# Splitting h straight from the normalised input, and three pieces of shift and scale added up on VectorE

## The chip, the cores and the metric

One core of one Trainium2 chip runs the whole program. The metric is the device time of one execution in microseconds (us).

## What is computed

One diffusion step of a single trunk layer, for 128 context tokens and 256 latent tokens (T = 384 in all) of 2048 channels. Each of the two token sets has its own conditioning vector, and from it six vectors of 2048 (shift 1, scale 1, gate 1, shift 2, scale 2, gate 2). All numbers are float32. The change is in the first three lines of the layer:

```python
def ada_modulation(cond, w_ada, b_ada):
    m = jax.nn.silu(cond) @ w_ada + b_ada
    return [p[:, None, :] for p in jnp.split(m, N_MOD, axis=-1)]
...
    sh1, sc1, g1, sh2, sc2, g2 = ada_modulation(cond, w_ada, b_ada)
    h = rms_norm(x, g_norm1) * (1 + sc1) + sh1
    proj = h @ w_in
    q, k, v, bg, cg, u = jnp.split(
        proj, [D_ATTN, D_ATTN + D_KV, D_ATTN + 2 * D_KV, D_ATTN + 2 * D_KV + D_CONV,
               D_ATTN + 2 * D_KV + 2 * D_CONV], axis=-1)
```

Behind them come attention and a short convolution, the output projection, a router and sixteen experts, whose weights (some 400 MB) are read once.

## The kernel before

**Matrix products in two parts.** h and the weights of the projections are each split into a high part (rounded to the narrower format fp32r) and a low part (the rest), and TensorE forms three products of the parts. For the weights `hi_part(u)` on ScalarE writes the high part of unit u (`w_part(u, 0)`) and `lo_part(u)` on VectorE subtracts it from the raw unit (`w_part(u, 1)`). Unit u of 1 MB holds two chunks of 128 rows of `w_in` for the queries, so units 0 to 7 serve the chunks k = 0 to 15; units 8 to 11 hold four chunks of keys and values each. For h, `hp[:, 0, k]` is the high part of chunk k and `hp[:, 1, k]` the low part, each 128 x 384.

**Shift 1 and scale 1 first.** They come in three blocks of channels: chunks 0 to 5, 6 to 11, and 12 to 15 (`BLOCKS`). The rows of `w_ada` for a block arrive in pieces (`PIECES`): 16 of 768 KB for each of the first two blocks (pieces 0 to 15, 16 to 31), and 8 of 1 MB, each with two chunks of 128 rows, for the last (pieces 32 to 39). TensorE multiplies a piece by the conditioning (`piece(n)` there) into bank 0 and adds one to `w_used`. Buffers are few: the load of piece n waits until `w_used` has reached `PIECE_FREE[n]`, or until the piece before it in its buffer has been read.

**The order around the change is written out by hand.** SyncE issues the loads in the order of `START_LOADS` (a number is a piece, "u5" is unit 5); each waits in the queue behind the one before. TensorE runs the query products chunk by chunk, each of three token tiles t = 0, 1, 2 with 6 matmuls of 512 columns, and behind (k, t) the pieces of `PIECES_AT`. When a block's pieces are multiplied, VectorE copies the rows out (`start_rows`), TensorE turns them (`turn_start`), and VectorE makes shift and gain of the block's chunks. Block 1 is turned behind (5, 1), block 2 behind (11, 0). Where TensorE would stand still in the first block, `idle_work` issues products that nobody reads: 5 behind each of the pieces 8 to 15 and 12 behind the first turn.

**h_block.** Both ScalarE and VectorE have a function of this name, called for each block. VectorE's `h_even` makes the even chunks of h in place in `xhatT`, ScalarE makes the odd ones in place and then copies both to the high parts; VectorE subtracts to get the low parts (`h_parts_ready`). The two chunks of a pair are made together. In between, behind the first pair, stands one `lo_part` (unit 1 in block 0, unit 4 in block 1) and its `hi_part`. Behind block 2, ScalarE issues seven small loads and then does `hi_part(7)`, for which `lo_part(7)` and the products of k = 14 wait.

## Time and profile before

| what | us |
|---|---|
| median of 3 runs | 1526.53 |
| lowest and highest | 1525.94, 1527.6 |
| the profiled execution, its own time | 1527.68 |
| its span | 1526.0 |
| TensorE busy | 1448.4 |
| VectorE busy | 602.4 |
| ScalarE busy | 255.1 |

All stretches below are in microseconds from the span's start. Queries are computed from 53.6 to 146.1, then come keys, values and the convolution with attention until about 570, the router around 596 to 603, and the experts to the end. A busy time of TensorE counts matmuls that overlap; what tells more is the start of a group of matmuls beside the start of the next.

### The profile page before, as it was taken

Reading aid. Unit: us, or ns where it says so; the run is one execution under the profiler, and the core shown is the slowest. Engines: PE = TensorE matmul, PEld = TensorE weight load, DVE = VectorE, ACT = ScalarE, POOL = GpSimd, SP = SyncE. Lnnn points to the kernel's source line nnn. Section 1 sums busy time; section 2 is a strip of 40 time slices with the busy share of each in tenths; the row PEclk is TensorE's granted clock in tenths of the full one; section 3 lists DMA queues with packets and bytes.
Section 4 is the critical chain, followed back from the end, with each engine's and each line's share of the span. In section 5 each row is a group of like instructions: output and inputs, shape, how many; then the busy total and the mean of one; then the engine's idle time right before and its main releaser. Section 6 shows DMA issues by size and latency. Waiting matters only on the chain.

```text
span 1526.0 us, 18551 instructions
## 1 busy us (share of the span) xinstructions
PE 1448.4 (95%) x7856; PEld 882.8 (58%) x7856; DVE 602.4 (39%) x1019; ACT 255.1 (17%) x358; POOL 26.7 (2%) x58
## 2 busy tenths in 40 slices
PE   6999999999999999999989989889889899999998
PEld 3667788888889997435425335335335335335433
DVE  4433977978768986101301301301301201211313
ACT  4223223333233223000000000000000000000200
POOL 0000000000000000000000000000000000000000
PEclk8999999999999999999999999999999999999999
DMA  9999788777787659999999999999999999999999
GB/s 373 403 392 328 263 325 315 267 258 262 277 293 274 220 192 367 368 434 432 431 431 432 429 433 431 433 431 429 435 429 433 431 433 432 428 433 430 432 421 344
DMA packets 99264, 572.48 MB, mean 375 GB/s; under 512 B 9533, under 2 KB 54533, under 8 KB 76677
## 3 DMA queue, kind: packets, MB, share of 16 engines
q1 hardware_dynamic: 87824, 520.14, 83.4%
q0 software_dynamic: 6912, 50.33, 8.6%
q10 hardware_dynamic: 4468, 1.14, 0.3%
q8 instruction: 45, 0.74, 0.2%
q14 instruction: 15, 0.11, 0.0%
HBM read 565.02 MB, written 6.55 MB: 375 GB/s over the span
## 4 chain that ended last, share of the span: by engine, by line
PE 67%; DMA 23%; DVE 5%; SPq 2%; issue 2%; ACT 1%; ACTq 0%; DVEq 0%
PE psum L638 65%; DMA ring<-in_w_up 19%; SPq L551 2%; DMA res<-in_w_ada 1%; DMA ring<-in_w_ada 1%; DVE res L1615 1%; DVE w_parts L1505 1%; DMA ring<-in_w_down 1%; SPq L441 1%; PE psum L648 0%; PE psum L824 0%; PE psum L1076 0%; DVE stat L1575 0%; DVE hid L1574 0%; PE psum L1046 0%
## 5 line engine op out<-in xcount | busy, mean ns | idle before, releaser
L638 PE MATMUL psum<-ring,hid 128*64 128x512 f32 x3024 | 681.2, 598 | 52.9 <-DMA ring<-in_w_up 39.7
L638 PEld LDWEIGHTS psum<-ring,hid 128*64 128x64 f32 x3024 | 240.8, 138 | 469.8 <-issue 411.7
L1941 DVE TENSOR_TENSOR hid<-psum,hid 128x512 f32<-128x512 f32 x16 | 11.1, 692 | 517.2 <-PE psum L638 517.2
L638 PE MATMUL psum<-h_parts,w_parts 128*128 128x384 f32 x1152 | 207.3, 337 | 1.3 <-DVE mix L1648 1.3
L638 PEld LDWEIGHTS psum<-h_parts,w_parts 128*128 128x128 f32 x1152 | 199.9, 188 | 5.1 <-issue 2.5
L1505 DVE TENSOR_TENSOR w_parts<-ring,w_parts 128x2048 fp32r<-128x2048 f32 x52 | 119.1, 2290 | 76.5 <-ACT w_parts L1205 76.3
L1205 ACT ACTIVATE w_parts<-ring 128x2048 fp32r<-128x2048 f32 x52 | 99.6, 1916 | 208.8 <-PE psum L638 177.9
L638 PE MATMUL psum<-w_parts,h_parts 128*128 128x512 f32 x432 | 103.9, 395 | 2.1 <-DVE h_parts L1549 1.3
L638 PE MATMUL psum<-ring,early 128*32 128x512 f32 (+4 forms) x694 | 96.5, 536 | 7.6 <-DMA ring<-in_w_ada 6.5
L638 PEld LDWEIGHTS psum<-w_parts,h_parts 128*128 128x128 f32 x432 | 79.5, 188 | 27.8 <-issue 10.3
L638 PEld LDWEIGHTS psum<-early,mix 128*128 128x128 f32 x768 | 86.6, 192 | 9.0 <-issue 9.0
L638 PE MATMUL psum<-early,mix 128*128 128x128 f32 x768 | 88.6, 276 | 0.8 <-DVE early L1886 0.8
L1421 ACT ACTIVATE hid<-psum 64x1024 f32<-64x1024 f32 x24 | 24.4, 1018 | 334.9 <-PE psum L638 334.7
L638 PE MATMUL psum<-hid 128*128 128x384 f32 (+1 forms) x248 | 77.7, 465 | 0.0
L1615 DVE SCALAR_TENSOR_TENSOR res<-res,early 128x2048 f32<-128x2048 f32 x30 | 69.2, 2346 | 11.3 <-issue 6.5
L638 PE MATMUL psum<-attn_parts,w_parts 128*128 128x384 f32 x384 | 68.3, 335 | 0.0
L638 PE MATMUL psum<-conv_parts,w_parts 128*128 128x384 f32 x384 | 67.9, 335 | 0.0
L638 PEld LDWEIGHTS psum<-attn_parts,w_parts 128*128 128x128 f32 x384 | 66.6, 188 | 1.1 <-issue 0.8
L638 PEld LDWEIGHTS psum<-conv_parts,w_parts 128*128 128x128 f32 x384 | 66.5, 188 | 0.8 <-issue 0.8
L1933 DVE SCALAR_TENSOR_TENSOR res<-psum,mod,res 128x128 f32<-128x128 f32 x192 | 63.0, 409 | 0.8
L638 PEld LDWEIGHTS psum<-hid 128*128 128x128 f32 x248 | 45.7, 190 | 30.4 <-issue 5.7
L1414 ACT ACTIVATE hid<-psum 128x512 f32<-128x512 f32 x16 | 9.6, 597 | 271.7 <-PE psum L1046 158.4
(216 smaller groups left out, 754.0 us busy)
## 6 DMA issues: line engine op xcount, KB each, us to landing
ring<-in_w_up SPq DMA_DIRECT2D x30, 4096.0 KB, 23.2
ring<-in_w_gate SPq DMA_DIRECT2D x28, 4096.0 KB, 29.9
ring<-in_w_down SPq DMA_DIRECT2D x26, 4096.0 KB, 30.0
ring<-in_w_ada POOLq DMA_DIRECT2D x48, 1024.0 KB, 7.5
ring<-in_w_in SPq DMA_DIRECT2D x36, 1024.0 KB, 8.1
ring<-in_w_ada SPq DMA_DIRECT2D x28, 768.0 KB, 15.5
res<-in_w_ada SPq DMA_DIRECT2D x16, 1024.0 KB, 6.2
ring<-in_w_out SPq DMA_DIRECT2D x16, 1024.0 KB, 5.6
```

The lines of the kernel that those rows point to most:

```text
L441: sp.dma_start(piece_buf(n).rearrange("p (m n) -> p m n", m=2), src).then_inc(piece_in[PIECE_SEM[n]], 16)
L551: sp.dma_start(tail_slot(b, e)[:, 2 * half:2 * half + 2, :], down_pairs(e, 1, half)[:, :, col:col + width])\
L638: return nc.tensor.matmul(out, lhsT, rhs, start=start, stop=stop, skip_group_check=True)
L1205: return nc.scalar.activation(out, in_, ACT.Copy)
L1414: nc.scalar.activation(act.rearrange("p (a b) -> p a b", a=4), bank[3 if first and e == 0 else 0][:, :].rearrange("p (b a) -> p a b", a=4) ...
L1421: last = nc.scalar.activation(y_sb[half][row:row + ES, :].rearrange("p (b n) -> p b n", b=2), psum[row:row + ES, 2:4, :], ACT.Copy, scale= ...
L1505: tt(w_part(u, 1), raw_unit(u), w_part(u, 0).bitcast(F32), ALU.subtract).then_inc(lo_ready, 1)
L1615: stt(added_up_3[n], chunk_3, cond[:, k, n:n + 1], added_up_3[n], ALU.mult, ALU.add).then_inc(add_done_3, 1)
L1933: last = stt(xT[:, k, lo:hi], bank[b][:, lo:hi], mod3[:, 5 * KC + k, n:n + 1], xT[:, k, lo:hi], ALU.mult, ALU.add)
L1941: tt(by_row, bank[1][:, :].rearrange("p (b a) -> p a b", a=4), by_row, ALU.mult).then_inc(act_ready, 1)
```

## The change

It has three parts. First, ScalarE no longer makes chunks of h in place: it writes the high part of every chunk straight from `xhatT` (scale, shift and rounding in one operation, one for the 128 context tokens and one for the 256 latent ones), while VectorE makes the same chunk in float32 in one of four places in `tmp` (`h_full`) and subtracts, also in two operations per chunk; TensorE's tile t = 0 waits for the context half alone. Second, pieces 33, 35 and 37 are no longer multiplied on TensorE: VectorE multiplies them by the two conditioning vectors and adds them up in `added_up_1` (`piece_add`), and TensorE sums the result over the partitions behind piece 39 (`piece_sums`). Third, there is less idle work: none behind piece 15, and 6 behind the first turn.

```diff
-    [24, 25, 26, 28] + list(range(33, 37))
-
-START_LOADS = [*range(12), "u0", *range(12, 19), "u1", *range(19, 24), "u2", *range(24, 28), "u3", *range(28, 34), "u4", 34, 35, "u5", 36, 37, "u6", 38, 39, "u7"]
+    [24, 25, 26, 28] + [33, 0, 34, 0]
+ADDS_FREE = {37: 4, 39: 8}
+
+PIECES_ADDED = [33, 35, 37]
+PIECES_USED = len(PIECES) - len(PIECES_ADDED)
...
-             (6, 2): [32, 33], (7, 2): [34], (8, 2): [35, 36], (9, 2): [37], (10, 2): [38, 39]}
+             (6, 2): [32], (7, 2): [34], (8, 2): [36], (10, 2): [38, 39]}
...
-IDLE_FROM, IDLE_PIECE, IDLE_H = 8, 5, 12
+SUMS_AT = (10, 2)
+IDLE_FROM, IDLE_PIECE, IDLE_H = 8, 5, 6
...
+            def piece_sums():
+                pe.wait_ge(ones_set, 3)
+                pe.wait_ge(piece_added, 4 * len(PIECES_ADDED))
+                width = BLOCKS[2][1]
+                for n in range(2):
+                    for j in range(4):
+                        at = j // 2 * width + j % 2 * width // 2
+                        last = mm(bank[0][32 * j:32 * j + 32, 0:width // 2], add_rows_of[:, 1 - n:33 - n], added_up_1[n][:, at:at + width // 2], False, n == 1)
+                last.then_inc(w_used, 1)
...
-                if n >= IDLE_FROM:
+                if IDLE_FROM <= n < PIECE_ENDS[0] - 1:
...
-                pe.wait_ge(h_parts_ready, k + 1)
                 for t in range(NT):
+                    if t < 2:
+                        pe.wait_ge(h_parts_ready, 2 * k + t + 1)
...
-                for k in range(first_k + 1, end_k, 2):
+                for k in range(first_k, end_k):
                     for n, (lo, hi) in enumerate(COLS):
-                        last = nc.scalar.activation(xhatT[:, k, lo:hi], xhatT[:, k, lo:hi], ACT.Identity,
-                                                    scale=gain[:, 0, k, n:n + 1], bias=mod3[:, k, n:n + 1])
-                    last.then_inc(h_act, 1)
-                    a.wait_ge(h_dve, k // 2 + 1)
-                    copy(hp[:, 0, k - 1, :], xhatT[:, k - 1, :]).then_inc(h_hi, 1)
-                    a.wait_ge(h_act, k // 2 + 1)
-                    copy(hp[:, 0, k, :], xhatT[:, k, :]).then_inc(h_hi, 1)
+                        nc.scalar.activation(hp[:, 0, k, lo:hi], xhatT[:, k, lo:hi], ACT.Identity,
+                                             scale=gain[:, 0, k, n:n + 1], bias=mod3[:, k, n:n + 1]).then_inc(h_hi, 1)
...
-                h_even(first_k)
-                for k in range(first_k, end_k, 2):
-                    if k + 2 < end_k:
-                        h_even(k + 2)
-                    for kk in (k, k + 1):
-                        v.wait_ge(h_hi, kk + 1)
-                        tt(hp[:, 1, kk, :], xhatT[:, kk, :], hp[:, 0, kk, :].bitcast(F32), ALU.subtract).then_inc(h_parts_ready, 1)
+                h_full(first_k)
+                for k in range(first_k, end_k):
+                    if k + 1 < end_k:
+                        h_full(k + 1)
+                    for n, (lo, hi) in enumerate(COLS):
+                        v.wait_ge(h_hi, 2 * k + n + 1)
+                        v.wait_ge(h_dve, 2 * k + n + 1)
+                        tt(hp[:, 1, k, lo:hi], h_full_at(k)[:, lo:hi], hp[:, 0, k, lo:hi].bitcast(F32), ALU.subtract).then_inc(h_parts_ready, 1)
                     if k == first:
                         lo_part(more)
...
+            def piece_add(m):
+                n = PIECES_ADDED[m]
+                v.wait_ge(piece_in[PIECE_SEM[n]], piece_landed(n))
+                chunks = piece_buf(n).rearrange("p (m k n) -> p k m n", m=2, k=2)
+                for kk, k in enumerate(PIECES[n][1]):
+                    for cond_n in range(2):
+                        out = added_up_1[cond_n].rearrange("p (m n) -> p m n", m=2)
+                        done = 4 * m + 2 * kk + cond_n
+                        if m + kk == 0:
+                            ts(out, chunks[:, kk], cond[:, k, cond_n:cond_n + 1], None, ALU.mult).then_inc(piece_added, 1)
+                        else:
+                            v.wait_ge(piece_added, done - 1)
+                            stt(out, chunks[:, kk], cond[:, k, cond_n:cond_n + 1], out, ALU.mult, ALU.add).then_inc(piece_added, 1)
+
+            piece_add(0)
             lo_part(5)
+            piece_add(1)
+            piece_add(2)
             lo_part(6)
             h_block(2, None, None)
```

The new order of loads (`START_LOADS`) ends with 36, 38, 37, unit 6, 39, unit 7 in place of 36, 37, unit 6, 38, 39, unit 7. The load of piece 37 waits until piece 33 has been added up, and that of piece 39 until piece 35 has.

On VectorE, these rows stood in block 1 of h_block before, from the last operation that makes chunk 8 of h onwards; the L1505 is the low part of unit 4, and the two L1549 ahead of it are the low parts of chunks 6 and 7.

```order
L1526 TENSOR_SCALAR mix<-mix,gain,mod 128x256
L1549 TENSOR_TENSOR h_parts<-mix,h_parts 128x384 [waits h_hi] x2
L1505 TENSOR_TENSOR w_parts<-ring,w_parts 128x2048 [waits hi_ready]
L1526 TENSOR_SCALAR mix<-mix,gain,mod 128x128
L1526 TENSOR_SCALAR mix<-mix,gain,mod 128x256
L1549 TENSOR_TENSOR h_parts<-mix,h_parts 128x384 [waits h_hi] x4
```

The same place on VectorE in the changed kernel: L1522 is the low part of unit 4, the two L1571 ahead of it are the halves of chunk 6, and those of chunk 7 come two operations behind it.

```order
L1545 TENSOR_SCALAR hid<-mix,gain,mod 128x256
L1571 TENSOR_TENSOR h_parts<-hid,h_parts 128x128 [waits h_dve,h_hi]
L1571 TENSOR_TENSOR h_parts<-hid,h_parts 128x256 [waits h_dve,h_hi]
L1522 TENSOR_TENSOR w_parts<-ring,w_parts 128x2048 [waits hi_ready]
L1545 TENSOR_SCALAR hid<-mix,gain,mod 128x128 [waits h_parts_ready]
L1545 TENSOR_SCALAR hid<-mix,gain,mod 128x256
L1571 TENSOR_TENSOR h_parts<-hid,h_parts 128x128 [waits h_dve,h_hi]
L1571 TENSOR_TENSOR h_parts<-hid,h_parts 128x256 [waits h_dve,h_hi]
```

So the low part of chunk 7 has moved from ahead of the low part of unit 4 to behind it.

Still on VectorE, this is what stands between block 1 and block 2 in the changed kernel, where before there were only the low parts of units 5 and 6 (L1522 here).

```order
L1590 TENSOR_SCALAR mix<-ring,early 128x1024 [waits piece_in8]
L1590 TENSOR_SCALAR mix<-ring,early 128x1024
L1593 SCALAR_TENSOR_TENSOR mix<-ring,early,mix 128x1024 [waits piece_added] x2
L1522 TENSOR_TENSOR w_parts<-ring,w_parts 128x2048 [waits hi_ready]
L1593 SCALAR_TENSOR_TENSOR mix<-hid,early,mix 128x1024 [waits piece_added,piece_in1]
L1593 SCALAR_TENSOR_TENSOR mix<-hid,early,mix 128x1024 [waits piece_added] x3
L1593 SCALAR_TENSOR_TENSOR mix<-ring,early,mix 128x1024 [waits piece_added,piece_in8]
L1593 SCALAR_TENSOR_TENSOR mix<-ring,early,mix 128x1024 [waits piece_added] x3
L1522 TENSOR_TENSOR w_parts<-ring,w_parts 128x2048 [waits hi_ready]
```

Twelve operations are new, four for each piece, and the low parts of both units stand behind some of them.

On SyncE's queue, these are the last loads of the start in the changed kernel (pieces 36, 38 and 37, unit 6, piece 39, unit 7; a piece is two loads).

```order
L454 DMA ring<-in_w_ada 128x2x512 [waits w_used]
L454 DMA ring<-in_w_ada 128x2x512
L454 DMA ring<-in_w_ada 128x2x512 [waits piece_added]
L454 DMA ring<-in_w_ada 128x2x512
L467 DMA ring<-in_w_in 128x2x1024 [waits lo_ready]
L454 DMA hid<-in_w_ada 128x2x512 [waits piece_added]
L454 DMA hid<-in_w_ada 128x2x512
L467 DMA ring<-in_w_in 128x2x1024 [waits lo_ready]
```

Where all of them waited for TensorE (`w_used`) or the low parts before, two pieces now wait for VectorE's adds, and unit 6 and unit 7 are queued behind them.

## Rows read from the trace of the kernel before

**Rows 1.** The page's first line.

```profile
span 1526.0 us, 18551 instructions
```

**Rows 2.** The chain that ended last, 86 to 151: start, us, what.

```profile
124.14 0.99 ACT mix L1254 x2
...
131.23 1.93 ACT w_parts L1205
...
133.18 2.30 DVE w_parts L1505
...
135.53 10.59 PE psum L638 x52
```

**Rows 3.** Timeline of TensorE: start, us, group of instructions, idle before it.

```profile
49.23 1.38 PE L638 MATMUL psum<-ident 128*128 128x128 f32 x10
50.45 0.49 PE L689 MATMUL psum<-ident,hid 128*128 128x128 f32 x3
...
53.60 4.33 PE L638 MATMUL psum<-w_parts,h_parts 128*128 128x512 f32 x18
...
86.49 1.50 PE L638 MATMUL psum<-ring,early 128*32 128x384 f32 x16
...
92.59 4.34 PE L638 MATMUL psum<-w_parts,h_parts 128*128 128x512 f32 x18 [1.27 <-DVE h_parts L1549]
96.87 1.93 PE L638 MATMUL psum<-ring,early 128*32 128x256 f32 x32
98.73 4.37 PE L638 MATMUL psum<-w_parts,h_parts 128*128 128x512 f32 x18
...
121.76 1.66 PE L638 MATMUL psum<-w_parts,h_parts 128*128 128x512 f32 x6
...
135.53 4.37 PE L638 MATMUL psum<-w_parts,h_parts 128*128 128x512 f32 x18 [0.84 <-DVE w_parts L1505]
```

**Rows 4.** Issues of L441 between 71 and 72 (pieces 30 and 31).

```profile
L441 SPq DMA_DIRECT2D ring<-in_w_ada x2: 368/814/1259, 70.9 to 71.6; - x2
...
DMA to landing us min/median/max: 13.9/14.5/15.2
```

**Rows 5.** Timeline of VectorE in block 1.

```profile
90.45 1.25 DVE L1526 TENSOR_SCALAR mix<-mix,gain,mod 128x128 f32<-128x128 f32 x4
91.89 1.03 DVE L1549 TENSOR_TENSOR h_parts<-mix,h_parts 128x384 fp32r<-128x384 f32 x2 [0.19 <-ACT h_parts L1205]
96.76 2.29 DVE L1505 TENSOR_TENSOR w_parts<-ring,w_parts 128x2048 fp32r<-128x2048 f32 x1 [3.85 <-ACT w_parts L1205]
```

**Rows 6.** Timeline of ScalarE and its queue (ACTq).

```profile
94.81 1.92 ACT L1205 ACTIVATE w_parts<-ring 128x2048 fp32r<-128x2048 f32 x1 [2.55 <-DMA ring<-in_w_in]
...
126.88 0.33 ACTq L1273 DMA_DIRECT2D hid<-in_cache_k  x1
127.16 0.51 ACT L1205 ACTIVATE h_parts<-mix 128x384 fp32r<-128x384 f32 x1
```

**Rows 7.** Groups of VectorE by form, 195 to 250: busy, mean ns.

```profile
L1615 DVE SCALAR_TENSOR_TENSOR res<-res,early 128x2048 f32<-128x2048 f32 x8 | 18.5, 2349 | 10.8 <-issue 6.5 <-DMA res<-in_w_ada 4.3
...
L1612 DVE TENSOR_SCALAR res<-res,early 128x2048 f32<-128x2048 f32 x2 | 2.5, 1281 | 0.0
...
L1628 DVE SCALAR_TENSOR_TENSOR hid<-hid,vecT 128x255 f32<-128x255 f32 x2 | 1.0, 478 | 0.0
```

**Rows 8.** Issues of L446 between 108 and 124 (piece 39).

```profile
L446 SPq DMA_DIRECT2D hid<-in_w_ada x2: 368/420/471, 109.5 to 109.9; - x2
...
DMA to landing us min/median/max: 4.6/5.3/6.0
```

**Rows 9.** Timeline of TensorE in the experts, 1140 to 1210.

```profile
1142.87 7.09 PE L638 MATMUL psum<-ring,hid 128*64 128x512 f32 x32 [2.62 <-DMA ring<-in_w_up]
...
1201.14 8.78 PE L638 MATMUL psum<-ring,hid 128*64 128x512 f32 x32 [2.54 <-DMA ring<-in_w_up]
```

**Rows 10.** Stretches: us, PE busy, PEld, DVE, ACT, POOL, clock, DMA share, GB/s.

```profile
793.20:795.00 1.80, 1.80 (x6) 0.57 (x8) 0.00 (x0) 0.00 (x0) 0.00 (x0) 0.50 0.97 419
```

More of the change, by code:

```diff
@@ L84 @@
 PIECE_FREE = [max(k - A_BUFS + 1, 0) for k in range(KC)] + [9, 10, 11, 12, 13, 14, 15, 16, 16] + [KC + k - B_BUFS + 1 for k in range(B_BUFS, KC)] + \
-    [24, 25, 26, 28] + list(range(33, 37))
-START_LOADS = [*range(12), "u0", *range(12, 19), "u1", *range(19, 24), "u2", *range(24, 28), "u3", *range(28, 34), "u4", 34, 35, "u5", 36, 37, "u6", 38, 39, "u7"]
+    [24, 25, 26, 28] + [33, 0, 34, 0]
+ADDS_FREE = {37: 4, 39: 8}
+PIECES_ADDED = [33, 35, 37]
+PIECES_USED = len(PIECES) - len(PIECES_ADDED)
+START_LOADS = [*range(12), "u0", *range(12, 19), "u1", *range(19, 24), "u2", *range(24, 28), "u3", *range(28, 34), "u4", 34, 35, "u5", 36, 38, 37, "u6", 39, "u7"]
 PIECES_AT = {(0, 2): [16, 17], (1, 2): [18, 19, 20], (2, 2): [21, 22], (3, 2): [23, 24, 25], (4, 2): [26, 27, 28, 29], (5, 0): [30, 31],
-             (6, 2): [32, 33], (7, 2): [34], (8, 2): [35, 36], (9, 2): [37], (10, 2): [38, 39]}
+             (6, 2): [32], (7, 2): [34], (8, 2): [36], (10, 2): [38, 39]}
 TURN_AT = {(5, 1): 1, (11, 0): 2}
+SUMS_AT = (10, 2)
 U_Q = 8
-IDLE_FROM, IDLE_PIECE, IDLE_H = 8, 5, 12
+IDLE_FROM, IDLE_PIECE, IDLE_H = 8, 5, 6
 ATT = 2
@@ L250, in build @@
         chunk_3 = res[:, 2 * D:3 * D]
+        added_up_1 = [mix[:, n * c_size // 2:(n + 1) * c_size // 2] for n in range(2)]
         x_copy = nc.dram_tensor("x_copy", (X_PARTS, P, X_PART), F32).ap()
@@ L332, in build @@
         piece_in = [sem(f"piece_in{n}") for n in range(B_BUFS)]
-        w_used = sem("w_used")
+        w_used, piece_added = sem("w_used"), sem("piece_added")
         start_rows_out, start_turned = sem("start_rows_out"), sem("start_turned")
@@ L351, in build @@
         gains_ready, mod_rows_out, mod_turned, mod_read = sem("gains_ready"), sem("mod_rows_out"), sem("mod_turned"), sem("mod_read")
-        h_dve, h_act = sem("h_dve"), sem("h_act")
+        h_dve = sem("h_dve")
         qkv_acc, qkv_out = sem("qkv_acc"), sem("qkv_out")
@@ L438, in piece_load @@
                     sp.wait_ge(w_used, PIECE_FREE[n])
+                if n in ADDS_FREE:
+                    sp.wait_ge(piece_added, ADDS_FREE[n])
                 if b < 2:
@@ L615, in _ @@
             nc.gpsimd.memset(add_rows_of[:, 2:33], 0.0).then_inc(ones_set, 1)
-            pool.wait_ge(w_used, len(PIECES))
+            pool.wait_ge(w_used, PIECES_USED + 1)
+            pool.wait_ge(piece_added, 4 * len(PIECES_ADDED))
             def ada_load(m, k, j, added=False):
@@ L755, in _ @@
                         piece(n)
+                    if (k, t) == SUMS_AT:
+                        piece_sums()
                     if (k, t) in TURN_AT:
@@ L1522, in gains, with h_full, h_full_at @@
                 v.wait_ge(gains_ready, done)
-            def h_even(k):
+            def h_full(k):
+                if k >= 4:
+                    v.wait_ge(h_parts_ready, 2 * (k - 3))
                 for n, (lo, hi) in enumerate(COLS):
-                    last = ts(xhatT[:, k, lo:hi], xhatT[:, k, lo:hi], gain[:, 0, k, n:n + 1], mod3[:, k, n:n + 1], ALU.mult, ALU.add)
-                last.then_inc(h_dve, 1)
+                    ts(h_full_at(k)[:, lo:hi], xhatT[:, k, lo:hi], gain[:, 0, k, n:n + 1], mod3[:, k, n:n + 1], ALU.mult, ALU.add).then_inc(h_dve, 1)
+            def h_full_at(k):
+                return tmp[:, k % 4 * T:(k % 4 + 1) * T]
             def h_block(b, first, more):
@@ L1531, in h_block @@
                 first_k, end_k = col // P, (col + width) // P
-                v.wait_ge(w_used, PIECE_ENDS[b])
+                v.wait_ge(w_used, PIECE_ENDS[b] if b < 2 else PIECES_USED + 1)
                 copy(start_rows[:, 0:width // 2], bank[0][:, 0:width // 2]).then_inc(start_rows_out, 1)
```

## Prediction

> **What bounds the kernel now.** I read first the chain that ended last, then the timelines of TensorE, VectorE and ScalarE up to 150 us, then how long loads took to land. The chain of 86 to 151 [rows 2] shows TensorE's matmuls as the bound up to about 124, then ScalarE's work on h, seven small loads on its queue, the high part of unit 7 (131.23) and its low part (133.18), and from 135.53 TensorE again. TensorE's own timeline [rows 3] has only two waits between 53.6 and 146: 1.27 us ahead of k = 6, and 0.84 us ahead of k = 14. Everything behind 146 starts from the end of the queries and is chained to it, and the weights of the experts can only flow once the router is through. So I carry a shift at the start of k = 14 one to one to the end. The forecast is therefore where k = 14 starts, before at 135.53.
>
> The profiled execution took 1527.68 around a span of 1526.0 [rows 1], 1.15 above the median of 1526.53. The sum is a difference against this execution, and I apply it to the median.
>
> **Block 0.** Piece 15 ends where its idle work begins, 49.23 [rows 3]. The turn came at 50.45, held by that idle work. Without it the turn comes behind the copy of the rows, which takes about half a microsecond: 0.5 us saved. Before, 3.15 us passed from the turn to k = 0 (53.60). Now the first thing needed is two pairs of operations and a half-width subtraction on VectorE, in place of a full chunk's copy and subtraction: by the rows of block 1, 1.25 plus about 0.3 against the 2.1 us from 90.45 to 92.59 [rows 3, 5], 0.6 us saved. So k = 0 starts 1.1 us earlier. Little of it lives: pieces 30 and 31 are issued at 70.9 and 71.6 and land 13.9 and 15.2 later [rows 4], so the last at 86.8, and the pair was multiplied from 86.49, each taking 0.75. TensorE would now come 1.1 us sooner and wait for piece 31: block 1 is finished 0.3 us earlier.
>
> **Block 1, the new wait.** From there k = 6 starts 0.3 + 0.6 = 0.9 us earlier, at 91.7. Its products take 4.35 and piece 32, now alone, 0.97 (half of the 1.93 of 96.87, [rows 3]), so TensorE wants k = 7 at 97.05. But the low part of chunk 7 now stands on VectorE behind the low part of unit 4, and unit 4 lands only at 94.81: ScalarE waited 2.55 us for it [rows 6]. No load ahead of it in the queue changes. The low part of the unit runs from 96.76 to 99.05 [rows 5], then chunk 8's two operations (half of 1.25) and the first half of chunk 7 (0.3): k = 7 starts at 99.95. That is a new wait of 2.9 us, and k = 7 starts 1.2 us later than the 98.73 of before.
>
> **From k = 7 to the sums.** Two more pieces, 35 and 37, are gone: -1.95. The sums are 16 matmuls of 256 columns like a piece: +0.95. Net +0.2 at the start of (11, 0), 121.76 before, if nothing waits.
>
> **VectorE and piece 39.** After 99.05, block 1 has four pairs to make (0.62 each) and five chunks to subtract in halves (between 0.5, half of the 1.03 in [rows 5], and 0.7; I take 0.58): VectorE is free at 104.4. An add of 1024 elements is in no row. It lies between 478 ns (255 elements) and 2349 ns (2048) [rows 7]; the slope between them is 1.04 ns per element, which gives 1.28, or about 1.22 back to back. The plain multiply lies between nothing and 1281 ns; I take 0.7. Then piece 33 takes 3.85 (to 108.25), the low part of unit 5 2.3 (110.5), piece 35 4.9 (115.4), piece 37 4.9 (120.3), the low part of unit 6 2.3 (122.6). Piece 39 is issued at 115.4 and 115.8, against 109.5 and 109.9 before. With the 4.6 to 6.0 us to landing of then [rows 8] it is there between 120.4 and 121.8. Less is in flight ahead of it, so I take 120.8. TensorE wants it at 120.1: 0.7 us late. The start of (11, 0) moves by 0.2 + 0.7 = +0.9, to 122.65. The adds end at 120.3, ahead of the sums, and the low part of unit 6 just before the copy of the rows, so neither adds anything. If the cover of piece 39 is thinner, each microsecond that its issue is late is a microsecond of the whole.
>
> **k = 14.** Before, TensorE was ready for it 0.84 before it could start; what it waited for was the high part of unit 7 behind ScalarE's seven loads. The first of these was issued at 126.88, before the last activation of h started at 127.16 [rows 6]: the queue runs ahead as soon as no wait is left. In the changed block 2 the eight activations have no wait but the first one's, so the loads can be issued while they run. They are worth at least 0.8 us of lead, and k = 14 then waits for nothing: -0.8. If the queue does not run ahead, eight activations take what two pairs and four copies did, and the 0.8 stays.
>
> The Trainium skill ("Advanced Engine Details and Errata", section Engine Queue Depths) gives ScalarE's queue eight entries. By that all eight activations would be queued at once and the loads issued 2.5 us or more sooner; the sum is the same, since TensorE itself is the limit there.
>
> **Sum.** +0.9 - 0.8 = +0.1 us at k = 14, so 1526.53 + 0.1 = 1526.6.
>
> **The rivals.** A measurement of this kernel can tell about 0.2%, 3.05 us.
>
> *The clock falls in the new wait.* TensorE stands still for 2.9 us ahead of k = 7. In the experts there are 11 waits of 2.2 to 2.63 us; behind 6 of them 32 matmuls took 7.09 us, behind the other 5 some 8.6 to 8.8 [rows 9], with a granted clock of 0.50 just behind one of them, the 1.2 GHz level [rows 10]. So a fall costs 1.7. It would delay TensorE past the landing of piece 39, whose 0.7 is then covered: +1.1, 1527.6. The new wait is longer than any of the eleven, but not by much: I give it 0.31.
> The Trainium skill ("TensorE: Matmul & The Clock Gate", Part 1) says that the clock halves when the array has been idle, and that the moment varies from run to run; the eleven waits agree, 5 to 6.
>
> *No run-ahead on ScalarE's queue.* The 0.8 stays: +0.9, 1527.4. Chance 0.09.
>
> *Slower: the adds are long.* If an add costs what the 2048-element one does (2.35, because its source is two strided rows), piece 39 is issued 2 x 1.13 + 4 x 1.13 = 6.8 us later and the sums wait for four more: about +10, 1537. It decides once an add takes over about 1.5 us (ten adds x 0.3 = 3 us). Against it: the price per element in [rows 7] is steady. Chance 0.10.
>
> *Faster: all that TensorE is spared counts.* 1.1 of block 0, and three pieces less the sums (2.9 - 0.95), give 3.05 us, and the 0.8 of k = 14 comes on top: 1522.7. It needs piece 31, unit 4 and piece 39 all to be no limit. Unit 4's landing speaks plainly against it. Chance 0.06.
>
> The forecast itself gets 0.44.
>
> **How the numbers follow.** The forecast's own spread: piece 39 on time (-0.7) to its latest landing (+1.0), and 0.8 for which execution is compared. The low end is 1526.6 - 0.7 - 0.9 = 1525.0. The high end takes in the clock, the missing run-ahead and the spread: 1527.6 + 0.5 + 0.8 = 1528.9. Outside are the adds, the fast case and tails: 2 in 10. Within 0.2% end the forecast, the clock and the queue: 0.84. Faster 0.06, slower 0.10.
>
> **What the profile would show.** A wait of TensorE ahead of k = 7 of about 2.9 us, released by VectorE's low part of h; VectorE busy almost without a hole from 99 to 122; adds of 1.2 to 1.3 us; piece 39 issued near 115.4; perhaps a short wait for it at 120; ScalarE's seven loads issued beside its activations, and no wait at k = 14, which starts within 1.5 us of 135.5. Wrong I would be if k = 7 starts before 98.7, if adds take over 1.5 us, or if a shift of the queries' end is not what arrives at the end.

## Result and profile after: slower by 0.3%

| what | before | after |
|---|---|---|
| median, us | 1527.56 (11 runs) | 1531.87 (11 runs) |
| lowest and highest | 1525.94, 1530.74 | 1530.0, 1535.72 |
| ratio, 95% interval | | 1.0030, 1.0022 to 1.0038 |
| the profiled execution | 1527.68 | 1530.1 |
| its span | 1526.0 | 1528.4 |

Forecast were 1526.6, 0.1 us more than the 1526.53 that before had in its first three runs, and a range of 1525.0 to 1528.9. Measured are 4.3 us more than before, so the time lies outside the range, on the slow side. The profiled execution of after is among its fastest, and its span is 2.4 us longer than that of before, not 4.3; for the rest, more executions were profiled below.

TensorE's timeline of after, the rows that answer to [rows 3] (start, duration, group, idle before it):

```profile
49.48 0.54 PE L708 MATMUL psum<-ident,hid 128*128 128x128 f32 x3 [0.68 <-DVE hid L1554]
...
52.14 4.36 PE L647 MATMUL psum<-w_parts,h_parts 128*128 128x512 f32 x18 [0.78 <-DVE h_parts L1571]
...
86.39 0.85 PE L647 MATMUL psum<-ring,early 128*32 128x384 f32 x8 [0.48 <-DMA ring<-in_w_ada]
...
91.29 4.37 PE L647 MATMUL psum<-w_parts,h_parts 128*128 128x512 f32 x18 [0.73 <-DVE h_parts L1571]
95.58 1.07 PE L647 MATMUL psum<-ring,early 128*32 128x256 f32 x16
99.44 5.87 PE L647 MATMUL psum<-w_parts,h_parts 128*128 128x512 f32 x18 [2.79 <-DVE h_parts L1571]
...
122.75 1.69 PE L647 MATMUL psum<-w_parts,h_parts 128*128 128x512 f32 x6
...
138.40 4.37 PE L647 MATMUL psum<-w_parts,h_parts 128*128 128x512 f32 x18 [2.81 <-DVE w_parts L1522]
```

(The 18 matmuls at 91.29 are those of k = 6, at 99.44 of k = 7, at 138.40 of k = 14.) Two rows differ in kind from before. k = 7 waits 2.79 us, where 2.9 was forecast, and its 18 matmuls take 5.87 us in place of 4.37. And k = 14 waits 2.81 us where no wait was forecast: it starts 2.87 us later than the 135.53 of before, though (11, 0) at 122.75 is only 1.0 late. From there the lateness travels: the router's product is issued at 602.31 against 599.78.

The granted clock, in two stretches of after behind the wait of k = 7 (columns as in [rows 10]; the clock is the third from the right):

```profile
99.40:101.00 1.60, 1.56 (x4) 1.27 (x5) 1.60 (x6) 0.40 (x1) 0.00 (x0) 0.50 1.01 396
101.00:103.00 2.00, 2.00 (x7) 1.56 (x6) 2.00 (x9) 0.00 (x0) 0.00 (x0) 0.60 0.97 359
```

The granted clock is 0.50, the 1.2 GHz level, directly behind the wait, and back at about 102.6 (0.60 is the mean of 1.6 us at 0.50 and 0.4 us at 1.00).

VectorE in after, from the low part of unit 4 to the adds of piece 37:

```profile
96.32 2.29 DVE L1522 TENSOR_TENSOR w_parts<-ring,w_parts 128x2048 fp32r<-128x2048 f32 x1 [4.84 <-ACT w_parts L1227]
98.53 0.66 DVE L1545 TENSOR_SCALAR hid<-mix,gain,mod 128x128 f32<-128x128 f32 x2
99.11 0.62 DVE L1571 TENSOR_TENSOR h_parts<-hid,h_parts 128x128 fp32r<-128x128 f32 x2
...
103.53 1.41 DVE L1590 TENSOR_SCALAR mix<-ring,early 128x1024 f32<-128x1024 f32 x2
104.86 2.47 DVE L1593 SCALAR_TENSOR_TENSOR mix<-ring,early,mix 128x1024 f32<-128x1024 f32 x2
...
115.24 4.87 DVE L1593 SCALAR_TENSOR_TENSOR mix<-ring,early,mix 128x1024 f32<-128x1024 f32 x4 [0.86 <-DMA ring<-in_w_ada]
```

The first half of chunk 7 (99.11) comes behind the low part of unit 4, and it is what k = 7 waited for. Four adds take 4.87 us, 1.22 each.

ScalarE and its queue in block 2 of after, and SyncE's queue ahead of it:

```profile
125.16 0.49 ACT L1276 ACTIVATE h_parts<-mix,mod,gain 128x128 fp32r<-128x128 f32 x1 [5.40 <-DVE gain L1537]
125.19 0.34 ACTq L1290 DMA_DIRECT2D hid<-in_cache_k  x1
...
128.30 0.71 ACTq L1296 DMA_DIRECT2D perm_vec<-in_g_norm  x1
129.04 4.96 ACTq L1298 DMA_DIRECT2D early<-in_w_router  x1
134.10 3.71 ACT L1227 ACTIVATE w_parts<-ring 128x2048 fp32r<-128x2048 f32 x2 [5.31 <-issue]
```

```profile
114.41 0.88 SPq L454 DMA_DIRECT2D hid<-in_w_ada  x2
115.33 7.45 SPq L467 DMA_DIRECT2D ring<-in_w_in  x3
122.82 0.98 SPq L477 DMA_DIRECT2D x_copy<-res  x2
```

The first small load is issued 0.03 us behind the first activation's start: the run-ahead is there. But the seventh, the router's, holds the queue for 4.96 us, so the high part of unit 7 begins at 134.10. Before, the same two rows were these:

```profile
130.38 0.76 ACTq L1281 DMA_DIRECT2D early<-in_w_router  x1
131.23 1.92 ACT L1205 ACTIVATE w_parts<-ring 128x2048 fp32r<-128x2048 f32 x1 [3.56 <-issue]
```

The earlier first issue did not help, and the high part came 2.87 us later, exactly what k = 14 lost. What is different at that time is the traffic. SyncE's queue before was this:

```profile
109.51 0.88 SPq L446 DMA_DIRECT2D hid<-in_w_ada  x2
110.44 8.92 SPq L459 DMA_DIRECT2D ring<-in_w_in  x3
119.40 2.80 SPq L469 DMA_DIRECT2D x_copy<-res  x2
```

Piece 39 is issued at 114.41 instead of 109.51, the first of units 7 to 9 behind it 4.9 us later, and the copies of x behind them 3.4 us later. In the share of the DMA queues from 128 to 130 (packets, MB, share; q0 is GpSimd's, q1 SyncE's, q10 ScalarE's) before had

```profile
q0 software_dynamic: 106, 0.75, 95.1%
q1 hardware_dynamic: 6, 0.02, 2.1%
```

and after has, in the same stretch,

```profile
q1 hardware_dynamic: 156, 0.51, 62.7%
q0 software_dynamic: 40, 0.33, 38.8%
q10 hardware_dynamic: 16, 0.02, 2.3%
```

Before, SyncE's loads were nearly through (6 packets); after, 156 of their packets move here. From 130 to 132 after has

```profile
q0 software_dynamic: 61, 0.50, 60.1%
q1 hardware_dynamic: 62, 0.25, 29.9%
q10 hardware_dynamic: 61, 0.06, 9.0%
```

The three queues move equal numbers of packets, and ScalarE's packets are the small ones (0.06 MB in 61). The router's load lets ScalarE's queue go at 134.00, when SyncE's queue, with 59 packets from 132 to 134 and 14 from 134 to 136, runs out; the other runs below show that this is not the rule. The Trainium skill ("DMA: Bandwidth & Descriptors", section Queues, rings and completion order) says that a DMA engine goes round the queues by packets; the 61, 62 and 61 agree, as far as the trace's packets are those of that page.

### The profile page after: what moved, and what is told of

It reads as the page before. It is cut to its first block, busy times and chain, and to the rows that moved or that the text cites. A ratio compares the mean times of both kernels' runs of the same rounds, so it can differ in the third digit from the quotient of the medians.

```text
span 1528.4 us, 18525 instructions
## 1 busy us (share of the span) xinstructions
PE 1444.2 (94%) x7802; PEld 879.3 (58%) x7802; DVE 620.6 (41%) x1063; ACT 255.2 (17%) x358; POOL 26.7 (2%) x58
## 4 chain that ended last, share of the span: by engine, by line
PE 64%; DMA 26%; DVE 5%; issue 2%; SPq 2%; ACT 1%; ACTq 0%; DVEq 0%
PE psum L647 62%; DMA ring<-in_w_up 19%; DMA ring<-in_w_ada 2%; DMA ring<-in_w_in 2%; DMA res<-in_w_ada 1%; SPq L559 1%; DVE res L1655 1%; DVE w_parts L1522 1%; DMA ring<-in_w_down 1%; ACT w_parts L1227 1%; PE psum L657 0%; PE psum L846 0%; PE psum L1098 0%; ACTq L1298 0%; DVE stat L1615 0%
## 5 line engine op out<-in xcount | busy, mean ns | idle before, releaser
L1522 DVE TENSOR_TENSOR w_parts<-ring,w_parts 128x2048 fp32r<-128x2048 f32 x52 | 118.9, 2289 | 63.9 <-ACT w_parts L1227 63.7
```

What stands on the lines that cost most here:

```text
L1522: tt(w_part(u, 1), raw_unit(u), w_part(u, 0).bitcast(F32), ALU.subtract).then_inc(lo_ready, 1)
```

## Experiments

Two theories were compared first. **Stall:** units 7 to 9, pushed 5 us later by the pieces that wait for VectorE, are still moving when ScalarE issues its small loads; the router's load then holds ScalarE's queue, and that sets k = 14. **Early waits:** k = 7's wait and the clock behind it delay the whole, and the stall is covered by it. All ratios are to before, with 95% intervals.

**Small loads, or the router's alone, behind the high parts.** In `small_late` the seven loads stand behind `hi_part(8)`, in `router_late` only the router's:

```diff
-            a.dma_start(wr, w_router[0].rearrange("(k p) e -> p k e", p=P)).then_inc(wr_in, 16)
-
             hi_part(7)
             hi_part(8)
+            a.dma_start(wr, w_router[0].rearrange("(k p) e -> p k e", p=P)).then_inc(wr_in, 16)
```

> The changed kernel with ScalarE's seven small loads moved from ahead of the high part of unit 7 to behind that of unit 8. All theories of the stalled queue: nothing is left in the queue ahead of the high part of unit 7, k = 14 waits for nothing and starts near 135.6 instead of 138.4, 2.8 us off the 4.3 us by which the changed kernel is slower, so +1.5 us against before. Rival (the loss is the clock's fall at k = 7 and what the runs vary in, the stall is covered elsewhere): k = 14 may start earlier, but the time stays within 1 us of the changed kernel's, +4 us against before.

> The changed kernel with only the router's load moved behind the high part of unit 8; the other six stay. If the time goes in the issue of that one load (4.96 us for its 2048 rows of 64 bytes), the high part of unit 7 starts near 129.1 and the kernel gains the same 2.8 us as with all seven moved. Rival (any load that comes seventh on a full queue is held): the sixth or the next one is held in its place and the gain is under 1 us.

Measured: `small_late` 1527.46, 0.9999 (0.9990 to 1.0008), where 1.5 us above before was expected; `router_late` 1527.61, 0.9996 (0.9987 to 1.0005). TensorE and ScalarE in `router_late`:

```profile
99.45 7.17 PE L647 MATMUL psum<-w_parts,h_parts 128*128 128x512 f32 x18 [2.85 <-DVE h_parts L1572]
...
125.65 15.23 PE L647 MATMUL psum<-w_parts,h_parts 128*128 128x512 f32 x66
```

```profile
129.56 0.60 ACTq L1296 DMA_DIRECT2D perm_vec<-in_g_norm  x1
130.26 1.92 ACT L1227 ACTIVATE w_parts<-ring 128x2048 fp32r<-128x2048 f32 x1 [0.23 <-issue]
```

The clock fell longer at k = 7 than in after (7.17 us), and yet the loss is gone: one group of 66 matmuls runs through k = 14 without a wait. (11, 0) starts at 124.03, 2.3 us later than before, and of that 1.0 is left behind k = 14 (the next piece is multiplied at 140.82, before at 139.83), in an execution 1.0 us above the kernel's median. Moving one load of 128 KB gives the 4.3 us back. This is the main evidence that in after it is the stall, and not the early waits.

**Piece 39 late, in the kernel before.** Nothing of the change; only the load of piece 39 waits for more of TensorE's work:

```diff
-    [24, 25, 26, 28] + list(range(33, 37))
+    [24, 25, 26, 28, 33, 34, 35, 38]
```

> The kernel before with one number changed: the load of piece 39 waits until pieces 36 and 37 are used (near 115.5) instead of 35 (109.5). Nothing else of the change is in it; units 7, 8 and 9 are queued behind that load and come 5 to 6 us later, as in the changed kernel. Theory (late loads fill the DMA engines from 120 to 136 and hold ScalarE's small loads): the seven small loads take 6 us or more to issue instead of 4.3, land in about 10 us instead of 5.6, the high part of unit 7 starts near 134, k = 14 near 138, 3 to 4 us slower than before. Rival (the stall belongs to what the change does on ScalarE, the run of eight activations without a wait): the small loads are issued as before, k = 14 near 136.5 (piece 39 lands near 121, TensorE waits for it by 0.5 to 1 us), at most 1 us slower.

Measured: 1531.52, 1.0021 (1.0012 to 1.0029). Its rows:

```profile
121.51 1.66 PE L638 MATMUL psum<-w_parts,h_parts 128*128 128x512 f32 x6
...
137.78 7.20 PE L638 MATMUL psum<-w_parts,h_parts 128*128 128x512 f32 x18 [3.32 <-DVE w_parts L1505]
```

```profile
129.66 3.73 ACTq L1281 DMA_DIRECT2D early<-in_w_router  x1
```

(11, 0) starts 0.25 us before its time in [rows 3], but the router's load holds the queue 3.73 us and k = 14 starts 2.25 late, its 18 matmuls taking 7.20 us (granted clock 0.50 from 137.78 to 141). Here piece 39 is issued at 115.26. The lateness of piece 39 and of the units queued behind it is enough for the loss.

**No run-ahead.** ScalarE waits for its last activation of h before the first small load:

```diff
+            a.wait_ge(h_hi, 2 * KC)
             a.dma_start(kc, cache_k[0, 0].rearrange("s h d -> s (h d)")).then_inc(cache_in, 16)
```

> The changed kernel with one wait more: ScalarE issues the seven loads only when its eight activations of block 2 are done, some 3 us later than in the changed kernel. Theory 1 (the DMA engines are full with unit 7, 8, 9, the copy of x and two pieces for gate 1, which VectorE's adds have pushed 3 to 5 us later): the first issue is near 128.7, the router's load is still held until about 134, k = 14 starts near 138.4, time as the changed kernel's. Theory 2 (issuing them early and close together fills the queue by itself): the router's load takes under 1 us as before, the high part of unit 7 starts near 133, k = 14 near 137.3, 1 us faster than the changed kernel.

Measured: 1533.92 (5 runs, 1529.66 to 1535.88), 1.0044 (1.0030 to 1.0058). The profiled execution is the fastest of the five. Its rows are those of theory 2: the router's issue at 131.88 takes 1.04 us, though piece 39 is as late as in after (114.40) and 32 packets of SyncE's queue move during that issue; the high part starts at 133.02, and k = 14 at 137.32 behind a wait of 2.96. So a late piece 39 does not always bring the long hold; when the seven are issued matters too. Issuing them later was no cure either, since the high part waits for them: the median is no better than that of after, and 4.3 us above this profile, which doesn't show why.

**The low part of unit 4 behind chunk 7.** In VectorE's `h_block(1, 6, 4)` the 6, the chunk behind which the low part stands, becomes 7, so that k = 7 needn't wait for it.

```diff
-            h_block(1, 6, 4)
+            h_block(1, 7, 4)
```

> The changed kernel with VectorE's low part of unit 4 behind chunk 7 instead of behind chunk 6. k = 7 waits for nothing (it starts near 96.6 instead of 99.44) and the clock does not fall there. Theory (piece 39, whose load hangs on VectorE's adds and not on TensorE, is the next limit, and behind it ScalarE's queue): the start of (11, 0) moves only from 122.75 to about 122.3, k = 14 stays near 138.4, the time within 1 us of the changed kernel's. Rival (the new wait and the clock are the loss): the start of (11, 0) and the time gain 2 to 4 us.

Measured: 1530.29, 1.0016 (1.0007 to 1.0025). k = 7 starts at 97.00 with no wait, 2.44 us sooner than in after, but the gain stops at piece 39:

```profile
120.51 1.09 PE L647 MATMUL psum<-hid,early 128*32 128x256 f32 x16 [3.32 <-DMA hid<-in_w_ada]
...
138.65 4.38 PE L647 MATMUL psum<-w_parts,h_parts 128*128 128x512 f32 x18 [1.89 <-DVE w_parts L1522]
```

The wait of 2.79 us has become one of 3.32 for piece 39, and the router's load still holds the queue 4.88 us. k = 14 is not earlier. The median is 1.6 us below that of after, with intervals that just overlap, so a small gain is neither shown nor excluded.

**The parts apart.** `split_only` is after with pieces, loads and order of before (ScalarE's high parts and VectorE's halves alone); `adds_only` is before with the added pieces alone. The core of each edit, `split_only` against after and `adds_only` against before:

```diff
-                    if (k, t) == SUMS_AT:
-                        piece_sums()
...
-            piece_add(0)
             lo_part(5)
-            piece_add(1)
-            piece_add(2)
```

```diff
+                    if (k, t) == SUMS_AT:
+                        piece_sums()
...
+            piece_add(0)
             lo_part(5)
+            piece_add(1)
+            piece_add(2)
```

> The changed kernel with the pieces as before: no adds on VectorE, all eight pieces of the last block on TensorE, loads in the old order; the new split of h and the shorter idle work stay. Theory (the adds are what makes it slower): k = 7 waits about 1.4 us until 99.45, the start of (11, 0) is near 122.5, loads come hardly later than before, the small loads are issued without a stall, k = 14 near 135.5: the same as before within 1 us. Rival (the order of VectorE's work and the clock are the loss): 3 us or more slower than before.

> The kernel before with only the three pieces moved to VectorE, with the new order of loads; h is split as before and the idle work is the old. Theory: no wait at k = 7, TensorE wants piece 39 near 118 and gets it near 119, the start of (11, 0) is near 121, but units 7, 8, 9 come 4 us later, the small loads are held, the high part of unit 7 starts 11.4 us behind (11, 0) as in the changed kernel, k = 14 near 136.7: 1 to 2 us slower than before. Rival (it needs both parts of the change for the loss): at least 0.7 us faster than before, since (11, 0) starts earlier.

Measured: `split_only` 1530.81, 1.0012 (1.0003 to 1.0020); `adds_only` 1533.07 (7 runs), 1.0026 (1.0015 to 1.0037). In both, piece 39 is issued near 111.9 and the router's load holds the queue: 2.98 us in `split_only`, and in `adds_only`

```profile
128.67 3.29 ACTq L1302 DMA_DIRECT2D early<-in_w_router  x1
```

Only in `adds_only` does TensorE pay for it: (11, 0) is 1.8 us earlier than before, and yet k = 14 starts at 136.35 behind a wait of 3.43, with 5.98 us for its 18 matmuls. `split_only` is slower by the other theory:

```profile
99.54 5.99 PE L639 MATMUL psum<-w_parts,h_parts 128*128 128x512 f32 x18 [1.95 <-DVE h_parts L1551]
...
124.14 1.66 PE L639 MATMUL psum<-w_parts,h_parts 128*128 128x512 f32 x6
...
137.69 4.38 PE L639 MATMUL psum<-w_parts,h_parts 128*128 128x512 f32 x18 [0.76 <-DVE w_parts L1502]
```

The wait at k = 7 and the clock behind it make (11, 0) 2.4 us late. k = 14 is 2.2 late, and its wait of 0.76 is no longer than before, so here the stall is covered. In both profiles (that of `split_only` is the slowest of 11, that of `adds_only` lies at its median) about as much again, 2.4 us, is lost near 250, at the product of the convolution that is read below: waits of 2.33 and 2.44 us, and 6.00 and 5.89 us for its 24 matmuls in place of 4.46. Why that wait is longer there was not looked into.

**Clock kept.** 18 matmuls (two for each of nine calls) that nobody reads, ahead of k = 7 and of k = 14:

```diff
+                if k in (7, 14):
+                    idle_work(9, 7)
```

> The changed kernel with 9 rounds of idle work (2.5 us of products that nobody reads, into a bank free by then) in the place of each of the two waits, ahead of k = 7 and ahead of k = 14; nothing else. Theory (the waits cost more than their length, since the clock falls behind them in a part of the executions, at k = 14 for 1.5 to 2.8 us; the profiled execution of the changed kernel was one where it did not fall there): granted clock 1 behind both waits, k = 14 still starts between 137.3 and 138.4, the median falls by 1.5 to 2 us to 1530 and the spread of the runs shrinks from 5.7 us to under 4. Rival (the rest of the loss comes from elsewhere): the same median as the changed kernel's, 1531.9.

Measured: 1533.86 (6 runs, 1530.25 to 1538.18), 1.0034 (1.0022 to 1.0045). At k = 7 it did what it should (wait 0.70, then 4.39 us). At k = 14 it missed: the router's issue took 5.80 us, and a wait of 3.07 was left behind the idle work. The profiled execution is the slowest of the six. The run says nothing on what the clock there costs.

**The same kernels profiled again.** Three more executions of after, one of before.

> The changed kernel as it is, one more profiled execution. Theory: the span varies with two things behind the seven loads, how long the router's load holds ScalarE's queue (4.96 us in the first profile) and whether the clock falls behind the wait at k = 14 (4.37 us for 18 matmuls there, or some 7.2). An execution with a fall should be 2.5 to 3 us longer than one with the same stall and none. Rival: the spread comes from the experts, 600 us on, and k = 14's start and clock are the same in all.

> As the look before: the time follows the router load's stall and the clock at k = 14 if the theory holds, and does not if the spread comes from the experts.

> As the looks before: at least one of the four profiled executions should show the clock fallen behind the wait at k = 14, if falls there explain why the median of 11 runs lies 1.8 us above the first profiled one.

> The kernel before as it is, one more profiled execution. Theory: its router load holds the queue under 1 us again, k = 14 starts within 0.5 us of 135.5 and its 18 matmuls take 4.4 us, since its wait is 0.84 us. Rival: its stall varies as much as in the changed kernel.

| execution | span | router's issue | k = 7: 18 matmuls | (11, 0) | k = 14: start | wait | 18 matmuls |
|---|---|---|---|---|---|---|---|
| before | 1526.0 | 0.76 | 4.37 | 121.76 | 135.53 | 0.84 | 4.37 |
| before, second | 1526.3 | 0.81 | 4.37 | 121.65 | 135.55 | 0.96 | 4.37 |
| after | 1528.4 | 4.96 | 5.87 | 122.75 | 138.40 | 2.81 | 4.37 |
| after, second | 1530.5 | 5.47 | 5.70 | 122.58 | 138.53 | 3.12 | 6.00 |
| after, third | 1530.7 | 5.57 | 6.00 | 122.99 | 138.98 | 3.15 | 5.80 |
| after, fourth | 1529.7 | 6.05 | 4.38 | 121.76 | 138.52 | 3.92 | 5.99 |

The fourth in its rows:

```profile
119.90 1.07 PE L647 MATMUL psum<-hid,early 128*32 128x256 f32 x16 [0.31 <-DMA hid<-in_w_ada]
...
121.76 1.69 PE L647 MATMUL psum<-w_parts,h_parts 128*128 128x512 f32 x6
...
138.52 5.99 PE L647 MATMUL psum<-w_parts,h_parts 128*128 128x512 f32 x18 [3.92 <-DVE w_parts L1522]
```

Its clock did not fall at k = 7, so (11, 0) starts where it did before, and still k = 14 is 3.0 late: in this kernel nothing ahead of (11, 0) decides it. The sum closes: on the mean of four, k = 14 starts 3.07 us later than the mean of before and its matmuls take 1.17 longer, 4.24 together. The wait of TensorE ahead of a product of the convolution near 250 (1.32 and 1.58 before, 0.96 on the mean after) gives 0.5 of it back. That leaves 3.75; the router's product is 3.8 late and the span 3.7 longer. Three of four had the clock fallen behind the wait of k = 14 and the first didn't, so its span is the shortest of the four, 1.3 to 2.3 us below the others.

**What holds the queue: the router's form or its place.** `router_first` issues the router's load first of the seven. `router_wide` keeps it seventh, but reads the same 128 KB as 128 rows of 1024 bytes instead of 2048 rows of 64; the router then works on permuted weights, so the results are not those of the layer and the experts get other shares of the tokens:

```diff
-            a.dma_start(wr, w_router[0].rearrange("(k p) e -> p k e", p=P)).then_inc(wr_in, 16)
+            a.dma_start(wr, w_router[0].rearrange("(p k) e -> p k e", p=P)).then_inc(wr_in, 16)
```

> The changed kernel with the router's load issued first of ScalarE's seven small loads instead of last. If the router's load is slow by its own form (2048 rows of 64 bytes), it takes several us here too, or the load behind it does, and the high part of unit 7 starts near 134 as before the edit: ratio to before 1.002 to 1.004. If what counts is being seventh while nothing has landed yet, the router's issue takes under 1 us in first place and the last load (the norm's vector) takes 4 to 6 us; the high part starts near 134 too, and only the place of the stall tells the two apart. A third reading, that a load issued at 125 finds the queues still short enough, gives a high part at 130 to 131 and no wait over 0.5 us at k = 14: ratio 0.999 to 1.001.

> The changed kernel with the router's 128 KB read in another layout, 128 rows of 1024 bytes instead of 2048 rows of 64 bytes, in the same seventh place; the router then works on permuted weights, so the experts' share of tokens is another, while the same weights are read. If the number of rows makes the stall: the seventh issue takes under 1 us, the high part of unit 7 starts near 130, k = 14 waits under 0.5 us, ratio 0.999 to 1.001. If its place as seventh does: the issue takes 4 to 6 us again and the ratio stays 1.002 to 1.004.

Measured: `router_first` 1537.36 (6 runs), 1.0068 (1.0053 to 1.0082); `router_wide` 1532.75 (5 runs), 1.0036 (1.0022 to 1.0050). ScalarE's queue in `router_first`, and then in `router_wide`:

```profile
125.19 0.39 ACTq L1290 DMA_DIRECT2D early<-in_w_router  x1
125.61 9.59 ACTq L1291 DMA_DIRECT2D hid<-in_cache_k  x1
135.22 2.18 ACTq L1292 DMA_DIRECT2D hid<-in_cache_v  x1
```

```profile
129.39 4.69 ACTq L1298 DMA_DIRECT2D early<-in_w_router  x1
134.18 3.75 ACT L1227 ACTIVATE w_parts<-ring 128x2048 fp32r<-128x2048 f32 x2 [4.99 <-issue]
```

Neither simple reading fits both runs. The router's own issue takes 0.39 us in first place, and the second load is held 9.59; with long rows in seventh place it still takes 4.69. Nor does the end of SyncE's traffic explain when the queue lets go. It does so at 134.0 to 134.6 in the four of after, at 134.1 in `router_wide` and 135.2 in `router_first`, as SyncE's packets run out. But in `split_only` SyncE's queue moves 6 packets in the whole 2.98 us of the hold, in `piece39_late` the queue lets go at 133.39 with 51 packets of SyncE's in the next microsecond, and in `small_late` the seventh load is not held among SyncE's packets (124 of them during its issue):

```profile
141.14 1.05 ACTq L1300 DMA_DIRECT2D early<-in_w_router  x1
```

The eleven profiles with a hold of 2.98 us or more have one thing in common: GpSimd's two loads of 1 MB are moving during it (112 to 257 packets). In the five kernels with all seven loads late, where GpSimd's queue is idle or nearly so, no issue takes over 1.72. But before has GpSimd's packets moving as well (35 in the 0.76 us of the router's issue) and is not held.

The issue time of piece 39 goes with the hold only in the main. With the router's load seventh and ahead of the high parts, its issue takes 0.8 us where piece 39 is issued by 109.5, 3.0 and 3.3 near 111.9, 4.88 at 113.6, and 4.69 to 6.05 from 114.3 to 114.8, but 3.73 at 115.26 and 1.04 in `no_run_ahead`. No reading tried here fits all of these, and no run changed GpSimd's loads alone. The Trainium skill ("Perfetto Trace Analysis", section DMA Instruction — HWDGE (DVE, Sync)) says of such issues that their time in the profile takes in the generation of the descriptors, and that a buffer for these can fill. That would fit a load held behind others that hardly move; but before, all seven were issued by 131.14 with none landed, and no run here shows how much such a buffer holds or whether SyncE's loads share it.

**Repairs.** `before_small_late` is before with the seven loads behind `hi_part(8)`, `adds_late` the same with the added pieces, `split_order_late` the split with that and with the order of `pair_order`, `small_late_order` the whole change with both. The edit that they share:

```diff
-            a.dma_start(kc, cache_k[0, 0].rearrange("s h d -> s (h d)")).then_inc(cache_in, 16)
...
             hi_part(7)
             hi_part(8)
+            a.dma_start(kc, cache_k[0, 0].rearrange("s h d -> s (h d)")).then_inc(cache_in, 16)
...
```

> The kernel before with the seven small loads behind the high part of unit 8, nothing else. Theory: the 0.84 us wait ahead of k = 14 goes, k = 14 starts at 134.7 instead of 135.5, 0.8 us faster (too little to be sure of). Rival (the small loads cost something wherever they stand, for they then compete with the loads for gate 1): no gain or a loss of up to 1 us.

> The kernel before with the three pieces on VectorE and the seven small loads behind the high part of unit 8. In the run with the adds alone (11, 0) started at 119.98 and k = 14 at 136.35. Theory: with no small loads in the way k = 14 follows 12.9 us behind (11, 0), at 132.9 to 133, 2.5 us ahead of before; 2.5 us faster than before (ratio 0.998), so the adds are worth that once their side effect is taken away. Rival (the late loads cost elsewhere too, in unit 7 itself or in the loads for gate 1 behind (14, 2)): under 1 us faster.

> The changed kernel without the adds, with the low part of unit 4 behind chunk 7 and the small loads behind the high part of unit 8. Theory: no wait but the 0.7 us ahead of k = 6; (11, 0) starts near 120.9 and k = 14 near 133.8, 1.7 us faster than before: what the new split gives alone once its wait is gone. Rival: piece 31 and the other landings hold TensorE, under 0.8 us more than the small loads alone give (before with only those moved: 1.3 us faster in the ratio).

> The whole change with both repairs (low part of unit 4 behind chunk 7, small loads late). Theory: TensorE reaches piece 39 at 117.1 and waits 3.3 us for it as in the run with the order alone, the clock falls behind that wait in a part of the executions, (11, 0) starts near 123, k = 14 near 136: within 1 us of before, slower than either part with its own repair. Rival: with both repairs the gains add up, 3 us faster than before.

| kernel | median, us | ratio, 95% interval | (11, 0) in the profile |
|---|---|---|---|
| `before_small_late` | 1526.35 | 0.9987 (0.9979 to 0.9996) | 121.24 |
| `adds_late` | 1526.39 | 0.9991 (0.9983 to 1.0000) | 122.52 |
| `split_order_late` | 1526.9 | 0.9991 (0.9982 to 1.0000) | 120.31 |
| `small_late_order` | 1528.41 | 1.0003 (0.9994 to 1.0013) | 120.30 |

None waits at k = 14. Only the first is faster than before beyond its interval, by 1.6 us between the medians and 2 by the ratio, and it has nothing of the change. With both repairs the whole change has the fastest profiled execution of all (span 1523.4), with 66 matmuls from 121.93 on, but its runs spread from 1523.95 to 1532.97, and its time can't be told from that of before. What makes them spread was not found. In `adds_late`, TensorE waits 1.85 us for piece 39, whose 16 matmuls of 256 columns then take 1.73 us in place of 1.07 (granted clock 0.58 from 119.1 to 121), so (11, 0) is later than before although fewer pieces are multiplied.

## Why the prediction was wrong

- **Block 0 and block 1: right.** k = 0 starts at 52.14, 1.46 sooner (forecast 1.1). TensorE waits 0.48 for piece 31, and k = 6 starts at 91.29 (forecast 91.7). One term was a little small on its own rows: piece 31 landed at 86.8 and had been multiplied from 86.49 + 0.75 = 87.24, so 0.4 was to be had there, not 0.3.
- **The new wait at k = 7: right.** 2.79 us, start 99.44 (forecast 2.9 and 99.95), 2.78 to 2.81 in all four executions. The rival of the clock came true in three of four, at 1.3 to 1.6 us; it was given 0.31 and priced at 1.7.
- **VectorE and piece 39: right in sizes.** Adds 1.22 each as taken, VectorE through with block 1 at 103.5 (forecast 104.4), piece 39 issued at 114.41 (forecast 115.4). Where the clock held, TensorE waited 0.31 for it (forecast 0.7). (11, 0) started at 121.76 to 122.99 (forecast 122.65).
- **k = 14: the step that failed.** The prediction said that the small loads "are worth at least 0.8 us of lead, and k = 14 then waits for nothing: -0.8". The loads were issued early, by 1.7 us, and k = 14 waited 2.81 to 3.92. The step took it for granted that the seven would be issued as quickly as before, 0.3 to 0.8 us each, though the same text had moved piece 39 by 5 us, and three units are queued behind piece 39. It priced that move at TensorE's wait for the piece alone, and never asked what the pushed units would meet. They met ScalarE's small loads. `router_late` takes the loss away and `piece39_late` makes it without the change. Term and measure: the wait ahead of k = 14 was to change by -0.8 and changed by +2.3 (3.25 on the mean of four against 0.90 of two). With the 0.8 by which (11, 0) is late on the mean, forecast as +0.9, that is the start of k = 14: 3.1 us late where +0.1 was forecast. Another +1.2 on the mean came from the clock behind that wait, which was in no rival.
- **The rival on the slow side** named a late piece 39, but with another cause (long adds), and priced it only as TensorE's wait. Its condition (adds over 1.5 us) was not met. The actual way to slower needed no long add.
- **The range.** Its low end takes 0.9 off where the text gives 0.8 for the execution compared; nothing hangs on it.
- **The shift is carried one to one: nearly, in after.** 0.5 of 4.2 us is absorbed at one wait near 250. In `split_only` and `adds_only` the same place added 2.4 us instead.

That issuing SyncE's loads later brings the stall is shown by `piece39_late`, and that the stall makes the loss by `router_late`. By what means ScalarE's queue is held, and whether SyncE's packets, GpSimd's or the small loads' own hold it, stays open.

## What to carry to other kernels

When a change delays a load, list every transfer that is queued behind it and ask which other engine issues DMAs at the time to which they move: an issue's duration in the old trace holds only for the old traffic. Small loads issued by an engine that also has work on the path are safer behind that work, unless they are needed at once; here that took the loss away and made even the kernel before a little faster. When the parts of a change are run alone, read for each which wait ends last: here both parts lost time, with the same long issue in both, but only one lost it by that issue. And a profiled execution that differs from the median by a large part of the effect should be profiled again before its rows are added up.

## What the runs showed of the hardware

- The issue of a small load on ScalarE's queue took 0.3 to 0.9 us in most rows. The seventh took 3 to 6 with GpSimd's loads in flight, mostly with SyncE's too, and a second load behind the router's 2048 rows took 9.59. With SyncE's loads alone in flight it took 1.05 (124 packets during the issue), and with GpSimd's alone, before, 0.76 (35 packets), but also 2.98 in `split_only` (142 packets, 6 of SyncE's).
- In such a hold the small loads crawl: 61 packets of ScalarE's queue from 130 to 132 in after, as many as of each other queue, against 2474 from 136 to 138, when the others were nearly through (19 and 2). They took 9.9 to 11.4 us from issue to landing, where they took 4.6 to 7.4 before.
- The clock fell behind waits of 1.85 to 3.92 us in some executions and not in others of the same kernel: at k = 7 in three of four with the same 2.8 us. 18 matmuls of 512 columns then took 5.7 to 7.3 us instead of 4.4.
